# Latent attention of a two-layer streaming encoder: both heads of a query tile in one step, and the last two output blocks late

## The reference

```python
def mla_attend(q, k_nope, k_pe, v, t0):
    s = (einsum('bqhd,bkhd->bhqk', qf[..., :128], k_nope)
         + einsum('bqhr,bkr->bhqk', qf[..., 128:], k_pe)) * (MLA_QK ** -0.5)
    mask = (tk[None, :] // CHUNK) <= (tq[:, None] // CHUNK)      # CHUNK = 64
    p = softmax(where(mask, s, NEG_BIG), axis=-1)
    return einsum('bhqk,bkhd->bqhd', p, v)

x = x + (silu(gate) * o) @ w_o_b          # per layer
y = rms_norm(x, g_final)
```

## Time and profile before

| | |
|---|---|
| median of 3 runs | 857.73 us (854.15 to 860.15) |
| span of the profiled execution, first to last instruction | 852.7 us |
| mean granted TensorE clock | 0.976 of full |
| PE busy | 809.2 us, 95% of the span |
| DVE, ACT, POOL busy | 449.7, 331.2, 314.0 us |
| attention of the second layer, four steps | 615.2 to 800.1 us |

### The profile page before, as it was taken

One profiled execution on the slowest core, in us unless ns is written; L12 is line 12 of the kernel. 1 busy time (PEld: TensorE's weight loads), 2 busy tenths in 40 slices (PEclk: granted clock), 3 DMA queues, 4 the chain that ended last, 5 costly groups with the idle time before them and its releaser, 6 DMA issues.

```text
span 852.7 us, 13543 instructions
## 1 busy us (share of the span) xinstructions
PE 809.2 (95%) x4623; PEld 659.0 (77%) x4623; DVE 449.7 (53%) x1023; ACT 331.2 (39%) x840; POOL 314.0 (37%) x261
## 2 busy tenths in 40 slices
PE   5699999999999999989999889999999999999996
PEld 4688888878787878746878878999777777765785
DVE  5556666666666676772135442115655555556322
ACT  6434333343333333341168333333444343446211
POOL 5345252525343444460123454434434232343100
PEclk9899999999999999967999999999999999999999
DMA  8531212030303030314032243230201002020211
GB/s 226 141 101 50 83 51 83 25 108 25 106 25 106 25 106 25 100 46 145 4 102 85 98 144 96 76 98 26 63 22 55 12 25 75 26 89 11 105 49 57
DMA packets 68082, 61.68 MB, mean 72 GB/s; under 512 B 7144, under 2 KB 55040, under 8 KB 68032
## 3 DMA queue, kind: packets, MB, share of 16 engines
q1 hardware_dynamic: 68032, 61.04, 23.4%
HBM read 50.85 MB, written 10.17 MB: 72 GB/s over the span
## 4 chain that ended last, share of the span: by engine, by line
PE 82%; DVE 6%; issue 5%; ACT 3%; POOL 2%; SPq 1%; DMA 1%; POOLq 0%; ACTq 0%; DVEq 0%
PE bank L416 17%; PE bank L418 17%; PE bank L417 17%; PE bank L676 5%; PE bank L968 3%; PE bank L710 3%; PE bank L688 3%; PE bank L1012 2%; PE bank L1014 2%; PE bank L1013 2%; PE bank L996 2%; PE bank L966 2%; PE bank L945 1%; DVE left L1753 1%; PE bank L980 1%
## 5 line engine op out<-in xcount | busy, mean ns | idle before, releaser
L1479 POOL TENSOR_TENSOR wlo<-raw,whi 128x1024 fp32r<-128x1024 f32 (+3 forms) x80 | 194.1, 2434 | 125.3 <-ACT whi L1098 125.0
L416 PE MATMUL bank<-whi,hthi 128*128 128x384 f32 (+1 forms) x360 | 129.4, 359 | 2.7 <-DVE wlo L1690 2.5
L417 PE MATMUL bank<-wlo,hthi 128*128 128x384 f32 (+1 forms) x360 | 125.6, 349 | 0.0
L418 PE MATMUL bank<-whi,htlo 128*128 128x384 f32 (+1 forms) x360 | 125.5, 349 | 0.0
L1098 ACT ACTIVATE whi<-raw 128x1024 fp32r<-128x1024 f32 (+3 forms) x84 | 82.4, 1008 | 32.8 <-PE bank L418 31.3
L1753 DVE TENSOR_TENSOR_SCAN left<-stay 128x512 f32<-128x512 f32 (+4 forms) x72 | 69.9, 971 | 20.7 <-ACT stay L1190 20.4
L1542 POOL TENSOR_TENSOR rstd<-msq,neg_half 128x4 f32<-128x4 f32 x40 | 40.3, 1007 | 100.6 <-DVE msq L1720 99.8
L416 PE MATMUL bank<-hthi,whi 128*128 128x272 f32 x256 | 75.0, 293 | 0.0
L416 PEld LDWEIGHTS bank<-whi,hthi 128*128 128x128 f32 x360 | 69.3, 193 | 6.9 <-issue 5.3
L418 PE MATMUL bank<-hthi,wlo 128*128 128x272 f32 x256 | 73.5, 287 | 0.0
L417 PE MATMUL bank<-htlo,whi 128*128 128x272 f32 x256 | 73.4, 287 | 0.0
(11 more groups left out here) (196 smaller groups left out, 1678.1 us busy)
## 6 DMA issues: line engine op xcount, KB each, us to landing
raw<-in_w_in_a SPq DMA_DIRECT2D x64, 256.0 KB, 3.1
raw<-in_w_in_b SPq DMA_DIRECT2D x24, 256.0 KB, 3.3
raw<-in_w_o_a SPq DMA_DIRECT2D x16, 256.0 KB, 2.8
raw<-in_w_kv_b SPq DMA_DIRECT2D x16, 256.0 KB, 3.1
raw<-in_w_o_b SPq DMA_DIRECT2D x16, 256.0 KB, 3.1
raw<-in_w_q_b SPq DMA_DIRECT2D x16, 192.0 KB, 2.4
x_in<-in_x_prompt SPq DMA_DIRECT2D x4, 512.0 KB, 5.1
out<-qkn SPq DMA_DIRECT2D x8, 256.0 KB, 2.4
```

The source lines that it names most:

```text
L416: eng.matmul(dst, st[0], mv[0], start=(k == 0), stop=False)
L417: eng.matmul(dst, st[0], mv[1], start=False, stop=False)
L418: mm = eng.matmul(dst, st[1], mv[0], start=False, stop=(k == n - 1))
L1479: nc.gpsimd.tensor_tensor(wlo[slot][:, c], raw[:, c], whi[slot][:, c].bitcast(F32), ALU.subtract).then_inc(s_lo, 1)
```

## The change

The units of a step are ordered by query tile: tile 3 of both heads, then tile 2, 1 and 0. An entry `("D", k)` takes the place of two entries `("S", u)`: TensorE makes the scores of units 2k + 1 and 2k + 2 together, first both key products, then both rotary products (head 0 on rows 0 to 63 of the array, head 1 on rows 64 to 127, into two banks), then both masks; VectorE takes both maxima, ScalarE both exponentials. An `("O", o)` with o > 0 now makes the values of one query tile for both heads, out of products of 128 columns. In `LAST_D` the entries H, E and F for head 6 are gone; ScalarE and VectorE split heads 6 and 7 behind the list, and TensorE adds heads 0 to 5 to both halves of tile 1 there before it finishes. The order of the other entries in both lists is new as well.

```diff
-UNIT_D = [None] + [(h, i) for h in range(2) for i in reversed(range(NT))]
+UNIT_D = [None] + [(h, i) for i in reversed(range(NT)) for h in range(2)]
+OD = 1 + NT
-STEP_D = [("Q", 0), ("P", 5), ("N", 0), ("K", 0), ("S", 0), ("N", 1), ("R", 0), ("Q", 1), ("X", 0), ("S", 1),
-          ("N", 2), ("Y", 0), ("R", 1), ("T", 0), ("K", 1), ("S", 2), ("N", 3), ("W", 0), ("R", 2), ("O", 0),
-          ("T", 1), ("Q", 2), ("S", 3), ("X", 1), ("N", 4), ("R", 3), ("K", 2), ("Y", 1), ("Q", 3), ("T", 2),
-          ("S", 4), ("N", 5), ("W", 1), ("R", 4), ("T", 3), ("X", 2), ("S", 5), ("N", 6), ("R", 5), ("T", 4),
-          ("K", 3), ("N", 7), ("Y", 2), ("S", 6), ("W", 2), ("R", 6), ("O", 1), ("T", 5), ("X", 3), ("Q", 4),
-          ("S", 7), ("R", 7), ("N", 8), ("T", 6), ("K", 4), ("Y", 3), ("N", 9), ("W", 3), ("S", 8), ("R", 8),
-          ("T", 7), ("K", 5), ("X", 4), ("N", 10), ("T", 8), ("Y", 4), ("O", 2)]
+
+STEP_D = [("Q", 0), ("P", 5), ("N", 0), ("K", 0), ("S", 0), ("N", 1), ("R", 0), ("Q", 1), ("X", 0), ("D", 0),
+          ("N", 2), ("Y", 0), ("R", 1), ("T", 0), ("K", 1), ("N", 3), ("W", 0), ("R", 2), ("O", 0), ("T", 1),
+          ("Q", 2), ("T", 2), ("X", 1), ("N", 4), ("D", 1), ("K", 2), ("Y", 1), ("R", 3), ("O", 1), ("N", 5),
+          ("Q", 3), ("R", 4), ("T", 3), ("T", 4), ("X", 2), ("W", 1), ("N", 6), ("D", 2), ("K", 3), ("R", 5),
+          ("Y", 2), ("N", 7), ("O", 2), ("Q", 4), ("R", 6), ("T", 5), ("T", 6), ("X", 3), ("W", 2), ("N", 8),
+          ("D", 3), ("K", 4), ("R", 7), ("Y", 3), ("N", 9), ("O", 3), ("W", 3), ("K", 5), ("R", 8), ("T", 7),
+          ("T", 8), ("X", 4), ("N", 10), ("Y", 4), ("O", 4)]
...
-          ("S", 0), ("R", 0), ("H", 0), ("W", 0), ("S", 1), ("R", 1), ("H", 1), ("T", 0), ("S", 2), ("R", 2),
-          ("E", 0), ("H", 2), ("W", 1), ("T", 1), ("O", 0), ("S", 3), ("R", 3), ("E", 1), ("H", 3), ("T", 2),
-          ("S", 4), ("R", 4), ("E", 2), ("F", 0), ("H", 4), ("W", 2), ("T", 3), ("S", 5), ("R", 5), ("E", 3),
-          ("F", 1), ("H", 5), ("T", 4), ("S", 6), ("R", 6), ("O", 1), ("E", 4), ("W", 3), ("T", 5), ("S", 7),
-          ("R", 7), ("E", 5), ("F", 2), ("T", 6), ("S", 8), ("R", 8), ("F", 3), ("T", 7), ("H", 6), ("F", 4),
-          ("F", 5), ("T", 8), ("E", 6), ("F", 6), ("O", 2)]
+          ("S", 0), ("H", 0), ("R", 0), ("D", 0), ("H", 1), ("W", 0), ("T", 0), ("E", 0), ("R", 1), ("H", 2),
+          ("R", 2), ("T", 1), ("T", 2), ("W", 1), ("O", 0), ("D", 1), ("E", 1), ("R", 3), ("H", 3), ("O", 1),
+          ("R", 4), ("F", 0), ("T", 3), ("T", 4), ("W", 2), ("D", 2), ("E", 2), ("R", 5), ("H", 4), ("O", 2),
+          ("R", 6), ("F", 1), ("T", 5), ("T", 6), ("W", 3), ("D", 3), ("E", 3), ("F", 2), ("R", 7), ("H", 5),
+          ("O", 3), ("R", 8), ("E", 4), ("T", 7), ("T", 8), ("F", 3), ("F", 4), ("E", 5), ("F", 5), ("O", 4)]
...
-        wt2, o = alias("wt2", [P, NT, SEQ], o)
+        wt2, o = alias("wt2", [P, 2, NT, 2, P], o)
...
+            def score_two(p, par, k):
+
+                i = NT - 1 - k
+                pe.wait_ge(s_expd, UA * p + 2 * k + 1)
+                n = (i + 1) * P
+                heads = [(h, SCR[(par + 1 + 2 * k + h) % 2][:, 0:n]) for h in range(2)]
+                for h, b in heads:
+                    pe.matmul(b, q2t[:, par, h, i * P:n], k2t[:, par, h, 0:n], start=True, stop=False)
+                for h, b in heads:
+                    r = slice(h * ROPE, (h + 1) * ROPE)
+                    pe.matmul(b, q2t[r, par, 2, i * P:n], kpet[r, 0:n], start=False, stop=True)
+                for h, b in heads:
+                    pe.matmul(b[:, i * P:n], ident_b[:, :], chunk_mask[:, :], start=False, stop=True,
+                              skip_group_check=True).then_inc(s_score2, 1)
...
-                for j in range(NT):
-                    mm = pe.matmul(OUT[:, j * P:SEQ], v2[:, par, o - 1, j, :], wt2[:, j, j * P:SEQ],
-                                   start=(j == 0), stop=(j == NT - 1))
+                i = NT - o
+                for h in range(2):
+                    for j in range(i + 1):
+                        mm = pe.matmul(OUT[:, h * P:(h + 1) * P], v2[:, par, h, j, :], wt2[:, i % 2, j, h, :],
+                                       start=(j == 0), stop=(j == i))
                 mm.then_inc(s_av2, 1)
...
-            for k in range(KD - 1):
-                last_product(1, 0, k)
+            for nh in range(2):
+                for k in range(KD - 2):
+                    last_product(1, nh, k)
             for t in range(TT):
                 for nh in range(2):
                     n = 2 * t + nh
                     if begun(n - 3):
                         pe.wait_ge(s_ysum, n - 3)
-                    for k in range(KD - 1 if n < 3 else 0, KD):
+                    for k in range(KD - 2 if t < 2 else 0, KD):
                         mm = last_product(t, nh, k)
                     mm.then_inc(s_yprod, 1)
...
+                        elif what == "D":
+                            exp_d(p, par, 1 + 2 * n)
+                            exp_d(p, par, 2 + 2 * n)
...
-            act.wait_ge(s_od2, 3 * MP)
+            act.wait_ge(s_od2, OD * MP)
+            gated_hi(KD - 2)
             gated_hi(KD - 1)
...
-                head = sg[:, 2 * p + o - 1, 0:SEQ]
-                v.tensor_tensor(head, OUT[:, 0:SEQ], head, ALU.mult).then_inc(s_od2, 1)
+                i = NT - o
+                heads = sg[:, 2 * p:2 * p + 2, i * P:(i + 1) * P]
+                v.tensor_tensor(heads, OUT[:, 0:2 * P].rearrange("p (h c) -> p h c", h=2), heads,
+                                ALU.mult).then_inc(s_od2, 1)
...
+                    elif what == "D" and att:
+                        max_d(p, par, 1 + 2 * n)
+                        max_d(p, par, 2 + 2 * n)
```

More of the change, by code:

```diff
@@ L946, in turn_qk @@
                 mm.then_inc(s_xp2, 1)
[L948 to L953, removed]
-                b = SCR[ub]
[L955 to L971, removed]
@@ new lines, in score_d @@
+            def score_d(p, par):
+                ub = par
+                if begun(UA * p - 1):
+                    pe.wait_ge(s_expd, UA * p - 1)
+                pe.wait_ge(s_xev2, CD * (p + 1))
+                b = SCR[ub]
+                for h in range(2):
+                    r, o = slice(h * ROPE, (h + 1) * ROPE), slice(h * SMP, (h + 1) * SMP)
+                    pe.matmul(b[o, 0:SKEY], q2t[:, par, h, SEQ:TOK], k2t[:, par, h, SEQ:KEYS],
+                              start=True, stop=False)
+                    mm = pe.matmul(b[o, 0:SKEY], q2t[r, par, 2, SEQ:TOK], kpet[r, SEQ:KEYS],
+                                   start=False, stop=True)
+                mm.then_inc(s_score2, 1)
@@ L983, in out_d @@
             def out_d(p, par, o):
-                if begun(3 * p + o):
-                    pe.wait_ge(s_od2, 3 * p + o)
-                pe.wait_ge(s_wtev2, UA * p + (1 if o == 0 else 1 + NT * o))
+                if begun(OD * p + o):
+                    pe.wait_ge(s_od2, OD * p + o)
+                pe.wait_ge(s_wtev2, UA * p + 2 * o + 1)
                 if o == 0:
@@ L1376, in chunk_d @@
                 if t == 0:
-                    if begun(3 * (q - 1)):
-                        act.wait_ge(s_av2, 3 * (q - 1))
+                    if begun(OD * (q - 1)):
+                        act.wait_ge(s_av2, OD * (q - 1))
                 nc.scalar.activation(v2[:, par, :, t, :], kv[:, :, 1, :], ACT.Copy).then_inc(s_act2, 1)
@@ L1409, in wtev_d @@
                 if u == 0:
-                    if begun(3 * p - 2):
-                        act.wait_ge(s_av2, 3 * p - 2)
+                    if begun(OD * (p - 1) + 1):
+                        act.wait_ge(s_av2, OD * (p - 1) + 1)
                     nc.scalar.activation(wts2[:, :, :],
@@ L1416, in wtev_d @@
                 h, i = UNIT_D[u]
-                if i == NT - 1:
-                    if begun(3 * p + 2 * h):
-                        act.wait_ge(s_av2, 3 * p + 2 * h)
-                nc.scalar.activation(wt2[:, 0:i + 1, i * P:(i + 1) * P],
+                if h == 0:
+                    used = OD * p + NT - i - 1 - (1 if i >= 2 else 0)
+                    if begun(used):
+                        act.wait_ge(s_av2, used)
+                nc.scalar.activation(wt2[:, i % 2, 0:i + 1, h, :],
                                      TRB[ub][:, 0:(i + 1) * P].rearrange("p (j c) -> p j c", j=i + 1),
@@ L1446, in step_d @@
                         elif what == "S":
-                            exp_d(p, par, n)
+                            exp_d(p, par, 0)
+                        elif what == "D":
+                            exp_d(p, par, 1 + 2 * n)
+                            exp_d(p, par, 2 + 2 * n)
                         elif what == "H":
                             act.wait_ge(s_proj2, CD * MP)
-                            act.wait_ge(s_od2, 3 * (MP - 1) + (2 if n == KD - 2 else 0))
+                            act.wait_ge(s_od2, OD * (MP - 1))
                             gated_hi(n)
@@ L1983, in gate_out_d @@
```

(3 more changed lines are left out.)

5 lines of the change are left out of this document (3 added, 2 removed).

## The result

The changed kernel took 882.87 us (median of 4 runs, 879.27 to 885.99) against 858.12 us (4 runs) for the kernel before on the same chip: ratio 1.028, interval 1.024 to 1.033, 24.75 us slower. Timed again later it took 875.9 us (6 runs) against 853.28 (17 runs of before beside them): 1.025, 1.021 to 1.030, 22.6 us slower.

A forecast was written before the change was run, and what follows sets the result against it. TensorE, busy 95% of the span, was taken to set the end. Full steps +8.9, last step +4.9 and clock +3.5 gave +17.3 us: 875 us from the 857.7 median, range 862 to 888.

The forecast's parts named there:

- the last step: Last step, no chunks to hide chains: 9.3 us of waits, +4.9 us net, and +3.5 us for a clock fall.
- Scores: Paired scores on TensorE: rotary products fully overlap, 8.2 for 11.5 us, 3.3 us saved a step, 13.3 in four.
- The rival without overlap: Paired scores: rotary products don't overlap; half overlap costs 1.0 per step, none 2.1; 879 to 884 us; chance 0.10.
- Half overlap: Paired scores: head 1's first record runs only beside head 0's second; 2.3 us saved per step instead of 3.3.
- Values: Value products on TensorE: 0 to +0.3 us a step for two more switches of queue entries, taken as +0.15.
- Waits in full steps: Full steps, TensorE idle for scaled rows: 1.95 us at T4, 2.0 at T6, 1.65 at T8, 0.5 for W0's subtraction.
- hidden waits: Rival: each R is done before TensorE asks, so only the work counts; 845 us; chance 0.10.
- half the waits: Rival: the real chain is shorter than 1.6 us and the clock holds; about 862 us, within 1%; chance 0.10.
- The clock: TensorE's clock falls behind D0 in the last step, +3.5 us (bounds 0 and +14); nothing counted in full steps.
- the rival with nine falls: Full steps: the clock falls behind each of nine 2 us gaps, some 1.5 us each, +13, 888 us; chance 0.12.
- Cover behind the list: Behind the last list: gating and splitting heads 6 and 7, about 3 us, hidden under 36 products of 8.3 us.
- E6: Output block that leaves the last step's list, as F6 does; done behind it at the same price, 0.7 us each.

The follow-up runs named there:

- the first experiment: Changed kernel with three swaps in STEP_D alone, R4 ahead of Q3, R6 ahead of Q4, R8 ahead of K5: 868.39 us, 1.016 against the kernel before.
- the tight lists: Changed kernel with new STEP_D and LAST_D, both scalings of a pair side by side ahead of the chunk's sums, W entries moved: 846.47 us, 0.991.
- the tight lists apart: The 846.47 us kernel with reordered STEP_D and LAST_D, each head's rotary product directly behind its own key product: 862.54 us, 1.010.
- both lists: Changed kernel with R ahead of the chunk in STEP_D and a reordered LAST_D together, paired scores kept: 857.37 us, 1.004.

## Why the prediction was right, point by point

875 us was forecast, 882.87 and, in the second timing, 875.9 measured. That is +17.3 us forecast, +24.75 and +22.6 measured; in the traces the second layer accounts for 22.4 and 20.7. That 875.9 lies so near 875 is luck: before's median was 853.28 there and not 857.7. The mechanism holds: the pairs save what was forecast, and waits for scaled rows, in the places that were named, cost more than that. Short was the last step.

- *Scores*: 3.00 us for the pair of 512 (forecast 3.01), 2.33, 1.69 and 1.06 for the smaller ones (2.36, 1.71, 1.10). Full overlap is what the rows show, and putting the products apart costs 3.7 us a step. The rival without overlap is excluded. Half overlap, as the prediction derives it from the rule of the Trainium skill, "TensorE: Matmul & The Clock Gate", Part 3 (matmuls start and end in program order), would be 1.6 us for two products of 1.06; the pair took 1.06. But what the trace contradicts is that derivation, and not the rule: read one by one, the four rotary records start at 629.846, 629.853, 630.379 and 630.386 us and end in the same order, two and two. So a record of one product ran beside one of the other, where the prediction had taken both of head 0 to come first. Which record is whose the trace doesn't tell. The records of L710 stand two and two in the same way (306.856 and 306.863, 307.016 and 307.023), so that row too didn't speak against the rule, as the prediction had it.
- *Values*: 1.71, 1.26, 0.81 and 0.37 us, 4.14 a step, where each of two heads took 2.21 before; the +0.15 wasn't needed.
- *Waits in full steps*: idle for 1.77 to 1.83, 1.81, 1.48 and 0.43 to 0.69 us, 5.5 a step. The forecast counted from start to start, and so does this: T3 starts at 648.84, its three products keep a pace of 0.11, T4 starts at 651.10, which leaves 1.93 (forecast 1.95); in the same way T6 is 1.97 (2.0), T8 1.64 (1.65). A wait costs some 0.17 us more than the idle time shows, since the last record before it overlaps nothing. The causes are shown for T4 and T6 by the first experiment. For T8 the changed kernel's own trace fits the sums of K5 as the cause: GpSimd's subtraction (668.75 to 670.86) is over more than 1 us before the scaling, which isn't held.

```profile
668.75 2.11 POOL L1495 TENSOR_TENSOR wlo<-raw,whi 128x896 fp32r<-128x896 f32 x1
...
671.97 0.29 DVE L1996 TENSOR_SCALAR prob<-prob,p_inv 128x128 f32<-128x128 f32 x1
```

 But the cure that this suggests isn't enough: moved ahead of the sums, the scaling runs into the subtraction, and 1.40 of 1.48 us stay, 0.8 of them for the lock.
- *Step*: 55.33 us measured, 55.15 forecast. The rivals of hidden waits and of half the waits are out.
- *The last step* is the term that was mis-sized. Forecast: +4.9 and +3.5 for the clock, 8.4 with the two moved blocks. Measured: 9.7 + 1.4 = 11.1, and 8.0 + 1.4 = 9.4 in the second trace. Its rows:

```profile
790.26 3.59 PE L970 MATMUL bank<-k2t,q2t 128*128 128x512 f32 x4 [0.93 <-ACT prob L1412]
...
793.78 1.17 PE L973 MATMUL bank<-kpet,q2t 64*128 64x512 f32 x4
...
797.90 0.72 DVE L2015 TENSOR_TENSOR glo<-sg,ghi 128x544 fp32r<-128x544 f32 x1 [1.46 <-ACT ghi L1438]
...
798.95 2.48 POOL L1495 TENSOR_TENSOR wlo<-raw,whi 128x1024 fp32r<-128x1024 f32 x1 [13.75 <-ACT whi L1108]
799.28 0.42 PEld L985 LDWEIGHTS bank<-ident,prob 128*128 128x128 f32 x4 [3.62 <-DVE prob L1996]
...
799.56 2.46 DVE L2015 TENSOR_TENSOR glo<-sg,ghi 128x544 fp32r<-128x544 f32 x1 [0.33 <-ACT ghi L1438]
...
802.66 0.71 PEld L985 LDWEIGHTS bank<-ident,prob 128*128 128x128 f32 x4 [2.97 <-DVE prob L1996]
```

 T1's wait is 3.19 (forecast 4.8), T2's 2.73 (forecast 1.3), T4's 0.22 (1.15), T6's 0.84 (1.2), T8's 0.81 (0.8). W0's subtraction was expected ahead of the scaling before T1; it began at 798.95 and held VectorE's split part at 799.56 for 2.46 us where the one before took 0.72, so that T2 paid. The sum of the waits was right to 2 us. Not seen at all: D0 waits 0.93 us for the exponential of S0, and in the first trace its first rows already ran at a lower clock (3.52 us for the keys instead of 1.82). All idle times of the step together are 9.3 us where before had 1.2, net 8.1 for the 8.0 forecast. The rest is the clock's: an estimate from these rows (11.1, less 8.1, less 0.17 for each of four waits, plus the 3.4 saved) gives it some 6 us in the first trace, and some 4 in the second, whose D0 ran at full clock; 3.5 were forecast.
- *The clock*: forecast in the last step alone. It fell there, and once more in a full step, where the second step is 1.6 us longer than the first (windows, columns as above):

```profile
718.00:720.00 2.00, 2.00 (x15) 1.66 (x14) 1.75 (x8) 1.66 (x3) 0.37 (x2) 0.70 0.00 0
720.00:722.00 2.00, 2.00 (x6) 1.52 (x6) 0.33 (x2) 0.81 (x4) 1.90 (x1) 0.50 0.00 0
...
801.00:805.00 4.00, 2.33 (x9) 1.88 (x10) 1.57 (x3) 1.19 (x2) 0.43 (x1) 0.50 0.00 0
805.00:809.00 4.00, 4.00 (x10) 2.25 (x12) 0.23 (x1) 0.35 (x1) 2.35 (x1) 0.50 0.00 0
```

 0.50 is 1.2 GHz. That one fall is not an accident of the run. In each of the nine traces of kernels with waits of 1.1 us or more in their full steps (both of the changed kernel among them), one of the three full steps is longer by 1.5 to 1.6 us than its like in the same trace or in the next kernel with that list; with the rotary products apart all three are, one of them twice. In the traces of before, the tight lists and the tight lists apart, none is. Which step it hits changes from run to run. "The 2 us gaps lie between chunks, I count nothing" was wrong by 1.6 us; the rival with nine falls was wrong by far more.
- *What is left*: 8.7 us of the first trace ahead of the second layer. One of the places, in both kernels' traces, with the same program:

```profile
170.00:210.00 40.00, 38.80 (x240) 32.09 (x241) 23.46 (x38) 12.16 (x32) 12.51 (x8) 0.91 0.25 71
```

```profile
170.00:210.00 40.00, 39.68 (x262) 33.05 (x261) 25.16 (x43) 15.23 (x39) 14.41 (x10) 1.00 0.25 71
```

 The clock was 0.91 in the one and 1.00 in the other. All four runs of the first timing had a mean clock of 0.959 to 0.965, the six of the second 0.968 to 0.974. In the second trace of the changed kernel the layer starts at 612.81, 2.4 us earlier than in before's. So these microseconds aren't the change's; why the clock differs in an unchanged stretch stays open.
- *Cover behind the list*: held, with half of it to spare. The 1.4 us more behind the list are the two blocks E6 and F6 that were moved there (0.7 each).

Where did the 13 us that the pairs save go? Into waits for scaled rows: 5.5 us in a full step and 7.8 in the last, all but T1's 3.2 us there for the second scaling of a pair. The old lists had one scaling at a time with a chunk behind it; the change doubled what has to be ready at once and left the entries of VectorE, ScalarE and GpSimd where the unit order had them.

## What to carry to other kernels

Joining two units on the bound engine doubles what its successor asks for at one moment: walk the in-order list of every other engine again, and put both producers ahead of any work that depends on the chunk standing between. A place in a shared list orders each engine against itself alone; a move of one entry moves it on every engine, so look at who is behind it on each. Measure the joined work and its order apart (here 3.7 us a step for the pairs and 6.0 us a step for the order, of opposite sign) before the idea is given up: the same pairs with tight lists gave 0.991.

## What the hardware showed beyond what was expected

- Two 32-bit rotary products of 512 columns on the two row halves, into two banks, took 1.06 us together, the same as one alone.
- A VectorE instruction with two inputs or a scaling beside a GpSimd subtraction of 2.1 to 2.5 us took 1.06 for 0.29 (scaling of 128 columns), 1.30 to 1.71 for 0.28 (cosine product) and 2.46 for 0.72 us (split of 544 columns). The mean scaling was 553 ns with both lists and 378 with tight ones.
- The scatter of one kernel's runs goes with its clock: in the last timing the kernel before took 849.4 us at a mean of 0.984 and 860.1 at 0.971.
- TensorE's clock stood at its lower level in the last step of the tight lists too, although TensorE was busy all 4 us, where before's last step kept 1.00 throughout. Up to 762.5 us windows show 1.00, from there on 0.53 and less. So it fell behind waits of 0.78, 0.45 and 0.56 us in the 5 us before, and just as a fourth, of 0.92, began:

```profile
764.00:768.00 4.00, 4.00 (x6) 1.18 (x6) 1.75 (x4) 0.44 (x1) 0.17 (x1) 0.50 0.00 0
```

 That fourth wait, for the exponential of S0, would be the next to take away, for its own 0.92 us; that the clock would then hold isn't shown, and neither was tried.
